# RWKV score output moved into the inverse, first output projection begun with six groups ready, first activation tiles in pairs

## What is computed

```python
mask = key_pos[None, :] < (start + jnp.arange(QBLOCK))[:, None]
log_keep = jnp.where(mask, jax.nn.log_sigmoid(-z), 0.0)
log_a = z + lax.cumsum(log_keep, axis=3, reverse=True)
a = jnp.exp(jnp.where(mask, log_a, -jnp.inf))
return jnp.einsum('bhqs,bhsd->bhqd', a, vf)          # stick breaking
...
S = (S * w_t[:, :, None, :] - s_kk[..., None] * (kk_t * a_t)[:, :, None, :]
     + v_t[..., None] * k_t[:, :, None, :])          # RWKV, per token
```

## Time and profile before

| | before |
|---|---|
| median of the three runs | 3052.69 us |
| the profiled execution | 3052.2 us, its span 3050.5 |
| PE busy / weight loads | 2962.2 (97%) / 2607.1 (85%) |
| DVE busy | 1798.3 (59%) |
| ACT busy | 1453.9 (48%) |
| DMA, mean over the span | 161 GB/s |
| mean granted PE clock | 0.990 |

### The profile page before, as it was taken

One profiled execution on the slowest core, in us unless ns is written; L12 is line 12 of the kernel. 1 busy time (PEld: TensorE's weight loads), 2 busy tenths in 40 slices (PEclk: granted clock), 3 DMA queues, 4 the chain that ended last, 5 costly groups with the idle time before them and its releaser, 6 DMA issues.

```text
span 3050.5 us, 55918 instructions
## 1 busy us (share of the span) xinstructions
PE 2962.2 (97%) x22084; PEld 2607.1 (85%) x22084; DVE 1798.3 (59%) x2375; ACT 1453.9 (48%) x2241; POOL 13.1 (0%) x28
## 2 busy tenths in 40 slices
PE   8999999999999999999999999999999999999997
PEld 8888887778888888889999997999977888888886
DVE  4655565575554555564666665566667545555555
ACT  4544544344343444434566664456654434444342
POOL 0000000000000000000000000000000000000000
PEclk9999999999999999999999999999999999999999
DMA  7333334455555555544334433544335555555553
GB/s 228 110 111 106 108 115 138 166 191 192 190 188 192 187 193 188 190 160 138 120 135 142 137 128 136 182 140 139 132 121 219 191 192 186 194 190 192 188 187 111
DMA packets 156999, 491.86 MB, mean 161 GB/s; under 512 B 15584, under 2 KB 50528, under 8 KB 155776
## 3 DMA queue, kind: packets, MB, share of 16 engines
q1 hardware_dynamic: 154032, 476.18, 45.9%
q0 software_dynamic: 2224, 11.69, 1.0%
q10 hardware_dynamic: 544, 1.05, 0.1%
HBM read 486.76 MB, written 2.10 MB: 160 GB/s over the span
## 4 chain that ended last, share of the span: by engine, by line
PE 91%; DVE 5%; ACT 2%; issue 1%; DMA 0%; ACTq 0%; DVEq 0%; SPq 0%
PE pp L420 45%; PE mp L420 11%; PE pp L404 8%; PE mp L404 8%; PE pp L406 4%; PE mp L406 4%; PE mp L810 1%; PE mp L774 1%; PE mp L758 1%; PE mp L750 1%; DVE wl L1356 1%; ACT wh L886 1%; PE mp L816 1%; PE mp L556 0%; PE mp L572 0%
## 5 line engine op out<-in xcount | busy, mean ns | idle before, releaser
L1356 DVE TENSOR_TENSOR wl<-raw,wh 128x1024 fp32r<-128x1024 f32 (+1 forms) x936 | 1101.3, 1184 | 853.3 <-ACT wh L886 850.3
L886 ACT CAST wh<-raw 128x1024 fp32r<-128x1024 f32 (+1 forms) x936 | 944.7, 1019 | 862.2 <-PE pp L420 287.4
L420 PE MATMUL pp<-aT,wh 128*128 128x256 f32 x4704 | 899.3, 291 | 6.0 <-DVE wl L1356 6.0
L420 PEld LDWEIGHTS pp<-aT,wh 128*128 128x128 f32 x4704 | 734.8, 192 | 21.4 <-issue 6.9
L420 PE MATMUL pp<-aT,wl 128*128 128x256 f32 x2352 | 666.7, 283 | 0.0
L420 PEld LDWEIGHTS pp<-aT,wl 128*128 128x128 f32 x2352 | 451.2, 192 | 0.0
L420 PE MATMUL pp<-wh,hTh 128*128 128x512 f32 x896 | 360.1, 402 | 7.9 <-DVE hTl L1610 6.0
L404 PE MATMUL pp<-aT,wh 128*128 128x512 f32 x1024 | 364.3, 400 | 0.8 <-issue 0.8
L404 PE MATMUL mp<-aT,wh 128*128 128x512 f32 x1024 | 360.0, 397 | 0.0
L420 PE MATMUL pp<-wh,hTl 128*128 128x512 f32 x896 | 350.8, 392 | 0.0
L420 PE MATMUL pp<-wl,hTh 128*128 128x512 f32 x896 | 350.3, 391 | 0.0
(11 more groups left out here) (301 smaller groups left out, 2674.1 us busy)
## 6 DMA issues: line engine op xcount, KB each, us to landing
raw<-in_w_dram SPq DMA_DIRECT2D x800, 512.0 KB, 3.3
raw<-in_w_dram SPq DMA_DIRECT2D x136, 384.0 KB, 3.5
ws<-in_ln_dram POOLq DMA_DIRECT2D x8, 1024.0 KB, 6.2
out_dram<-xres SPq DMA_DIRECT2D x8, 256.0 KB, 2.0
ws<-in_lora_dram POOLq DMA_DIRECT2D x8, 192.0 KB, 3.5
xres<-in_x_dram ACTq DMA_DIRECT2D x2, 512.0 KB, 6.1
xres<-in_x_dram SPq DMA_DIRECT2D x2, 512.0 KB, 7.0
ws<-in_c_dram POOLq DMA_DIRECT2D x1, 576.0 KB, 7.1
```

What stands on the lines that cost most here:

```text
L420: last = mm(o, lhs, rhs, start=opens and m == 0, stop=end and kk == 1 and m == 2, skip_group_check=True)
L886: nc.scalar.copy(wh[:, q % RING, :, 0:width], raw[:, q, :, 0:width]).then_inc(S("hi_ready"), 1)
L1356: tt(wl[:, q % RING, :, 0:width], raw[:, q, :, 0:width], f(wh[:, q % RING, :, 0:width]), ALU.subtract).then_inc(S("lo_ready"), 1)
```

## The change

1. **Score output.** `sb_o` is no step of its own. The two matmuls now stand in level 4 of the inverse behind `dX`, write bank 1 of `mp` in place of bank 3, and wait for `attn` (long set) and for the second `tok_ready`. ACT copies `BK` out of bank 1 one level earlier each, and copies `sb_o` in level 4; DVE makes its low part in level 5, where one of the seven pieces of the next group's token shift stood, which goes behind the loop. `XAV` waits for `sb_lo`, the Gram step no longer. The list loses a step, and the shares of the steps 0 to 3 are (3, 3, 3, 3).
2. **Output projection.** PE begins it with `mix0_out` of 6 and asks for 7 before unit 6 (`late`). Its mixer goes by `HOPS0Z`: shares (2, 2, 2, 2), then as before, and 4 in the last step; the sum is 31.
3. **First tiles.** For k = 0 the tiles go in four pairs on all three engines; ACT and DVE split the first two units behind the first pair. The waits for `xlo` stay.

```diff
-HOPS0 = (3, 3, 2, 2, 2) + 16 * (1,) + (0, 1, 0, 1, 0, 1, 1)
+HOPS0 = (3, 3, 3, 3) + 16 * (1,) + (0, 1, 0, 1, 0, 1, 1)
+HOPS0Z = 4 * (2,) + HOPS0[4:-1] + (4,)
+TILES = tuple((range(2 * y, 2 * y + 2) for y in range(4))), (range(0, 4), range(4, 6), range(6, 8), ())
...
+            def late(one, u_late, name, seen):
+                def held(u, half=None):
+                    if u == u_late and half == 0:
+                        pe.wait_ge(S(name), seen)
+                    one(u, half)
+                return held
...
-                for y, tiles in enumerate((range(0, 4), range(4, 6), range(6, 8), ())):
+                for y, tiles in enumerate(TILES[min(k, 1)]):
                     for r in tiles:
                         turn(r)
 
                     pe.wait_ge(S("xlo"), 8 * k + 2 * y + 2)
                     yield
...
-                pe.wait_ge(S("attn"), m1)
-                mm(mb[3][:, 0:T], vtk[:, 0, :], sba[:, 0:T], ...)
-                mm(mb[3][:, P:T], vtk[:, 1, :], sba[:, T:384], ...).then_inc(S("sb_o"), 1)
-                yield
                 pe.wait_ge(S("operands"), m1)
-                pe.wait_ge(S("sb_lo"), m1)
...
                     last.then_inc(S("dX"), 1)
+                    if lv == 4:
+                        pe.wait_ge(S("attn"), m1)
+                        pe.wait_ge(S("tok_ready"), 2 * m1)
+                        mm(mb[1][:, 0:T], vtk[:, 0, :], sba[:, 0:T], ...)
+                        mm(mb[1][:, P:T], vtk[:, 1, :], sba[:, T:384], ...).then_inc(S("sb_o"), 1)
                     yield
...
-                pe.wait_ge(S("tok_ready"), 2 * m1)
+                pe.wait_ge(S("sb_lo"), m1)
...
-            pe.wait_ge(S("mix0_out"), GROUPS - 1)
-            drive(blocks(P_OUT0, B_OUT0, ..., per=7), 28, 0, mix0(GROUPS - 1), HOPS0)
+            pe.wait_ge(S("mix0_out"), GROUPS - 2)
+            drive(late(blocks(P_OUT0, B_OUT0, ..., per=7), 6, "mix0_out", GROUPS - 1), 28, 0,
+                  mix0(GROUPS - 1), HOPS0Z)
```

More of the change, by code:

```diff
@@ L510, in mix0 @@
                 yield
-                pe.wait_ge(S("attn"), m1)
-                mm(mb[3][:, 0:T], vtk[:, 0, :], sba[:, 0:T], start=True, stop=False, skip_group_check=True)
-                mm(mb[3][:, P:T], vtk[:, 1, :], sba[:, T:384], start=False, stop=True,
-                   skip_group_check=True).then_inc(S("sb_o"), 1)
-                yield
                 pe.wait_ge(S("operands"), m1)
-                pe.wait_ge(S("sb_lo"), m1)
                 to_tiles()
@@ L574, in mix0 @@
                     last.then_inc(S("dX"), 1)
+                    if lv == 4:
+                        pe.wait_ge(S("attn"), m1)
+                        pe.wait_ge(S("tok_ready"), 2 * m1)
+                        mm(mb[1][:, 0:T], vtk[:, 0, :], sba[:, 0:T], start=True, stop=False, skip_group_check=True)
+                        mm(mb[1][:, P:T], vtk[:, 1, :], sba[:, T:384], start=False, stop=True,
+                           skip_group_check=True).then_inc(S("sb_o"), 1)
                     yield
@@ L650, in _ @@
             drive(group0(GROUPS - 1), 2 * UNITS, 0, mix0(GROUPS - 2), HOPS0)
-            pe.wait_ge(S("mix0_out"), GROUPS - 1)
-            drive(blocks(P_OUT0, B_OUT0, "A", H, (0, 1, 0, 1), WIDE, per=7), 28, 0, mix0(GROUPS - 1), HOPS0)
+            pe.wait_ge(S("mix0_out"), GROUPS - 2)
+            drive(late(blocks(P_OUT0, B_OUT0, "A", H, (0, 1, 0, 1), WIDE, per=7), 6, "mix0_out", GROUPS - 1), 28, 0,
+                  mix0(GROUPS - 1), HOPS0Z)
             pe.wait_ge(S("mix0_out"), GROUPS)
@@ L852, in _ @@
                 drive(group1(P_L1 + 3 * g + 3, B_L1 + 3 * g + 3, 1 - g % 2), 3 * UNITS, 0, mix1(g, True), HOPS1W)
[L854 to L861, removed]
             pe.wait_ge(S("mix1_out"), 7)
-            drive(out1(P_OUT1A, B_OUT1A, (1, 0, 1, 0), UNITS, 6, 8), 4 * UNITS, 0, mix1(4, True), HOPS1W)
+            drive(late(blocks(P_OUT1A, B_OUT1A, "A", H, (1, 0, 1, 0), WIDE), 6, "mix1_out", 8), 4 * UNITS, 0, mix1(4, True), HOPS1W)
             drive(group1(P_L1B, B_L1B, 1), 3 * UNITS, 0, then(12), HOPS_SOLO)
@@ L869, in _ @@
             pe.wait_ge(S("mix1_out"), 13)
-            drive(out1(P_OUT1B, B_OUT1B, (0, 1, 0, 1), 6, 4, 14), 24, 0, mix1(7, True), HOPS1W)
+            drive(late(blocks(P_OUT1B, B_OUT1B, "A", H, (0, 1, 0, 1), WIDE, per=6), 4, "mix1_out", 14), 24, 0, mix1(7, True), HOPS1W)
             pe.wait_ge(S("mix1_out"), 16)
@@ L888, in new_x @@
             def new_x(k):
-                for tiles in (range(0, 4), range(4, 6), range(6, 8), ()):
+                for tiles in TILES[min(k, 1)]:
                     for r in tiles:
@@ L898, in new_x @@
                                        r2(mb[r % 4][:, :], a=4)).then_inc(S("xhi"), 1)
-                    if k == 0 and tiles == range(0, 4):
+                    if k == 0 and tiles == range(0, 2):
                         for q in range(LEAD):
@@ L980, in mix0 @@
                 yield
-                act.wait_ge(S("sb_o"), m1)
-                nc.scalar.copy(hTh[:, bass.ds(m * 2, 1), :], mb[3][:, 0:T].unsqueeze(1)).then_inc(S("sb_hi"), 1)
-                yield
                 yield
@@ L997, in mix0 @@
                 for lv in range(1, 6):
-                    if lv == 2:
+                    if lv == 1:
                         st(nc.scalar.copy(BK[half(0), :, :], r2(mb[1][half(0), :], a=4)))
+                    elif lv == 2:
+                        st(nc.scalar.copy(BK[half(1), 1:4, :], r2(mb[1][half(1), 0:3 * P], a=3)))
                     elif lv == 3:
-                        st(nc.scalar.copy(BK[half(1), 1:4, :], r2(mb[1][half(1), 0:3 * P], a=3)))
-                    elif lv == 4:
                         nc.scalar.copy(BK[half(1), 0, :], mb[1][half(1), 3 * P:4 * P]).then_inc(S("tok_ready"), 1)
@@ L1006, in mix0 @@
                     nc.scalar.copy(XTf0, mb[0][:, 0:T]).then_inc(S("XT_ready"), 1)
-                    if lv == 5:
+                    if lv == 4:
+                        act.wait_ge(S("sb_o"), m1)
+                        nc.scalar.copy(hTh[:, bass.ds(m * 2, 1), :], mb[1][:, 0:T].unsqueeze(1)).then_inc(S("sb_hi"), 1)
+                    elif lv == 5:
                         act.wait_ge(S("AV"), m1)
@@ L1081, in _ @@
             interleave(mix0(GROUPS - 2), HOPS0, *group0(GROUPS - 1, last=True))
-            interleave(mix0(GROUPS - 1), HOPS0, 28, wide(P_OUT0), (), nothing, True, begun=True)
+            interleave(mix0(GROUPS - 1), HOPS0Z, 28, wide(P_OUT0), (), nothing, True, begun=True)
             st.leave_straight()
@@ L1369, in low @@
                     tt(aTl[:, ks, ts_], r2(mb[r % 4][:, :], a=4), f(aTh[:, ks, ts_]), ALU.subtract).then_inc(S("xlo"), 1)
+                if k == 0:
+                    for tiles in TILES[0]:
+                        for r in tiles:
+                            low(r)
+                        if tiles == range(0, 2):
+                            for q in range(LEAD):
+                                split(0, q, NARROW)
+                        yield
+                    return
                 norm(0)
@@ L1375, in new_x @@
                     low(r)
-                if k == 0:
-                    for q in range(LEAD):
-                        split(0, q, NARROW)
                 yield
@@ L1534, in mix0 @@
                 yield
[L1535 to L1538, removed]
                 dve.wait_ge(S("gram"), m1)
@@ L1559, in mix0 @@
                        ALU.mult).then_inc(S("Yn"), 1)
-                    if lv > 2:
+                    if lv == 5:
+                        dve.wait_ge(S("sb_hi"), m1)
+                        tt(hTl[:, bass.ds(m * 2, 1), :], mb[1][:, 0:T].unsqueeze(1), f(hTh[:, bass.ds(m * 2, 1), :]),
+                           ALU.subtract).then_inc(S("sb_lo"), 1)
+                    elif lv > 2:
                         next(pieces, None)
@@ L1569, in mix0 @@
                     yield
+                next(pieces, None)
                 next(pieces, None)
@@ L1644, in _ @@
             interleave(mix0(GROUPS - 2), HOPS0, 2 * UNITS, narrow(2 * GROUPS - 1, True), (), nothing, True, True)
-            interleave(mix0(GROUPS - 1, False), HOPS0, 28, wide(P_OUT0), *out_hook(P_OUT0, B_OUT0, (0, 1, 0, 1), 7, 0, True, False), True,
+            interleave(mix0(GROUPS - 1, False), HOPS0Z, 28, wide(P_OUT0), *out_hook(P_OUT0, B_OUT0, (0, 1, 0, 1), 7, 0, True, False), True,
                        begun=True)
```

## The result

The changed kernel took 3061.19 us (median of 8 runs, 3057.4 to 3066.12), the kernel before 3050.65 in the 8 runs beside it: ratio 1.0035, 95% interval [1.0025, 1.0044], so 10.7 us slower by the ratio. The profiled execution took 3062.84 (span 3061.1), 10.6 above that of before. Lines of the file moved: L420 of before is L422, L1356 is L1358, L512 is L582.

The account below looks back on a forecast made before the run. PE, busy 97% of the span, was taken as the bound, so time could come only from its gaps, clock or work; 4.2 + 9.6 - 8.1 + 4.7 + 3.0 = 13.4 on 3052.2 gave 3066 us, range 3054 to 3072.

Parts of the forecast that it names:

- Groups, +13.8 forecast: Seven groups: score output costs PE 0.6 each, +4.2, and six clock falls of 1.6 cost +9.6.
- The step held for the most certain: Groups: PE's wait for the exponential becomes a 2.35 wait for unit 5's split; Gram starts as before, gain 0.
- six of seven fell, as taken: Groups: the new gap of 2.35 brings the clock down in six of seven, 6 x 1.6 = +9.6.
- Projection, -8.1 forecast: Output projection: waits of 3.36 and 2.68 go with their slow clock, a 1.4 wait for unit 6 comes; -3.8 and -4.3.
- Start, +7.7 forecast: First tiles: PE begins 1.5 earlier, waits 1.8 three times, one more pair costs 0.8: +4.7; clock +3.0.
- the +3.0 for the clock: Start: two of the three pair waits of 1.8 bring the clock down, 2 x 1.5.
- (a): Rival: the clock holds in the groups and pairs, sum +0.8, 3053 us; chance 0.15.
- (b): Rival, groups: unit 5's split arrives before 322.4, old waits really go, groups -5.6, no falls, 3043 us; chance 0.06.
- (c): Rival: every gap brings the clock down, the wait for unit 6 included, +19.4, 3072 us; 0.13 shared with (d).
- (d): Rival, projection: the wait moves to another split, the clock falls there, -8.1 shrinks to about -3, 3071; 0.13 with (c).

Follow-up runs that it names:

- early_split: The changed kernel with unit 5's split moved on ACT and DVE to mixer step 1, ahead of the long chain: 3039.06 us, ratio to before 0.9964.
- filled_wait: The changed kernel with three spare matmuls of constants on PE ahead of unit 5 in each of seven groups: 3054.41 us, ratio to before 1.0013.
- before_early: The kernel before with only unit 5's split made early on ACT and DVE, score output still its own step: 3059.09 us, ratio 1.0027.
- start_only: The kernel before with only the first activation tiles changed to four pairs: 3055.55 us, ratio 1.0016.
- proj_only: The kernel before with only the output projection change, begun with six groups ready and its shares fitted to the older list: 3042.87 us, ratio 0.9976.
- groups_only: The kernel before with only the score output moved to level 4 of the inverse, shares 3, 3, 3, 3: 3069.37 us, ratio 1.0062.
- start_better: The changed kernel with PE's old tile order (four, two, two) and the first two units split right behind the first pair of tiles: 3052.61 us, ratio 1.0005.

## Why the prediction was right, and where its sizes were off

The sum had +13.4, the profiled execution has +10.6 and the ratio +10.7: the direction, the stages and their signs came out, and each stage within about 1.5.

**Groups, +13.8 forecast, +13.2 measured.** The step held for the most certain held: the wait of L512 turned into a wait of 2.33 (2.35 forecast) for unit 5, and early_split shows that this split makes it. A group with no fall took 60.19, against 59.53 in the trace of before: `sb_o` costs 0.66, 0.6 forecast. A fall costs 1.45 by filled_wait, 1.6 forecast. That just six of seven fell, as taken, was luck: the forecast had one gap of 1.77 to go by, and in the same place in layer 1 two of the ten traces show no fall.

**Projection, -8.1 forecast, -8.9 measured.** Both old waits went with the slow clock behind them, the new one is 1.36 (1.4 forecast) and left the clock alone. The size depends in part on the execution of before that it is held against: in before_early, which has the same projection, the wait of 2.68 brought no fall, and the stage took 127.41 in place of 128.81.

**Start, +7.7 forecast, +6.2 measured.** Without the clock's share +4.7 was forecast; measured it is 5.3, which is 6.2 less 0.9 (below). The pairs are as summed: from the first transpose of a pair to the next matmul of the weights 22.37 - 19.77 = 2.6 in place of 0.8, three times. (The trace gives the wait as 1.56, since it counts from the modelled end of the transposes.) PE began 1.1 earlier, not 1.5, in part as the first weights landed 8.3 behind their issue, not 8.0; x itself landed 0.9 later in this execution than in the one of before (8.60 against 7.68). The term that failed is the +3.0 for the clock: none of the three pair waits brought it down, where I had taken two of three from the one gap of 1.77 that did. Instead the matmuls from 13.03 to 18.3 went at half pace, which costs 0.9 more than the slow stretch of before, and which I had not forecast. That the pairs make it isn't shown: start_only, with the same start, was slow to 16.2 only and lost 5.1 in all, and proj_only, with the start of before, was slow from 14.25 to 19.4. So a term of +3.0 that didn't come was in part made up by one that nobody had summed.

**The rivals.** (a), the clock holds: filled_wait shows what that would be worth, and it didn't hold. (b) needed the split ahead of half 10; it doesn't come there by itself. Moved there by hand it makes the groups 10.1 shorter than before, where (b) had 5.6. Its price left out a term: with the split early, the 0.92 that `sb_o` takes in its old place (323.60 to 324.52) goes too, and only the 0.66 in its new place comes. In figures 7 x (0.66 + 0.24 - 2.35) = -10.2. (c) and (d) needed the fall at unit 6, which didn't come. The rule of the Trainium skill ("TensorE: Matmul & The Clock Gate", HAM oscillation — how this bites in real kernels), by which gaps as short as these leave the clock alone, is not borne out: of 28 waits of 1.9 and 2.3 in the groups of four of these traces, 25 were followed by 1.2 GHz.

## What to carry to other kernels

When a wait is first in a list, look what PE, or whichever engine bounds, needs next, and when that is ready: the wait for the exponential covered a wait for a weight split that ended only 1.2 us later, and taking away the first alone bought nothing. Price such a move from the point where the engine stops to the point where it goes on, with the work between counted in. In this schedule by hand, the order of splits against long mixer steps on the helping engines was worth 23.2 in the groups with PE's own order untouched; the two lists needn't be the same. Idle gaps of PE near two microseconds should be summed with the clock that they cost, here 1.45 beside 2.3, and filled where they can't be removed.

## What the runs showed of the hardware that I had not expected

Gaps of PE of over 1.1 between matmuls, in all ten traces, and how many of them were followed by 1.2 GHz. The wait for the very first weights and those of over 4 us at the layer norms are left out:

| gap | where | times | followed by 1.2 GHz |
|---|---|---|---|
| 1.15 to 1.18 | groups, for the exponential | 21 | 0 |
| 1.36 | projection, for unit 6 | 5 | 0 |
| 1.44 | layer 1 | 10 | 0 |
| 1.56 | first tiles, behind a pair of transposes | 12 | 0 |
| 1.75 to 1.77 | layer 1 | 10 | 8 |
| 1.88 to 1.90 | groups of before_early | 7 | 7 |
| 2.32 to 2.35 | groups, for unit 5 | 21 | 18 |
| 2.65, 2.68 | projection | 5 | 3 |
| 3.35 to 3.37 | projection | 4 | 4 |

No gap up to 1.56 brought the clock down in these traces. From 1.75 on most did, but not every one, and the same gap in the same place brought it down in one execution and not in another.

Which of the seven waits goes by follows an order. In the changed kernel the slow clock began 0.6, 0.4 and 0.1 behind PE's return in the first three groups, then 0.1, 0.3 and 0.4 ahead of it, and the seventh wait went by. In groups_only it came 0.4 ahead in the fourth group, the fifth went by, and in the sixth it came 0.8 behind; in start_better the fifth went by in the same way. That six of seven holds for another spacing of the waits isn't shown: in before_early, with 61.2 from wait to wait, it was seven of seven.

At the start the column of the granted clock can't be taken at its word: in the changed kernel the window from 13 to 20 us shows 1.00, while its matmuls run at the pace of 1.2 GHz until 18.3 (0.63 a pair). The first record of the clock in that trace stands at 18.35. The durations tell it, the clock column doesn't.
